# The mixer of a two-block network: its projection in three passes, weights streamed through four slots

## The reference

```python
proj = rms_norm(x) @ w_in                  # 1024 -> 2560: q, k, v, g, u
ret  = silu(g) * retention(rope(q), rope(k), v)   # chunks of 128 tokens, 8 heads
pool = (window_mean(u) - u) @ pool_w[g] * pool_scale   # 4 groups of 128 channels
h    = x + concat(ret, pool) @ w_out
# then h + moe(rms_norm(h)): logits, top 4 of 32 experts
```

## Time and profile before

| | us |
|---|---|
| median of 3 runs (lowest, highest) | 5710.15 (5708.48, 5718.44) |
| profiled execution | 5713.9 |
| its span, first to last instruction | 5712.2 |

### The profile page before, as it was taken

How to read it: one execution, slowest core, us unless ns; L and a number is a source line. 1 busy time by engine, 2 the same in 40 slices (tenths; PEclk the granted TensorE clock), 3 DMA queues, 4 the chain that set the end, 5 groups by cost and what they waited for, 6 DMA issues and landing times. The chain is left out here.

```text
span 5712.2 us, 77504 instructions
## 1 busy us (share of the span) xinstructions
PE 5329.2 (93%) x24921; PEld 3492.1 (61%) x24922; DVE 3181.3 (56%) x5954; ACT 2149.6 (38%) x3222; POOL 633.2 (11%) x865
## 2 busy tenths in 40 slices
PE   8999999499999999999999999789996599999788
PEld 4555555366666666666666666455654477777455
DVE  4434333567676767777777777443434544434176
ACT  3111111144444445555555555232222533333154
POOL 0000000100000000000000000100000199200000
PEclk9999999699999999999999999899998799999899
DMA  4112111356564647677777777333232300000433
GB/s 145 52 55 73 51 51 51 131 166 196 162 199 159 201 157 234 228 235 236 236 237 236 235 238 237 139 121 116 91 116 74 116 5 6 7 8 7 157 122 108
DMA packets 424923, 770.33 MB, mean 135 GB/s; under 512 B 57361, under 2 KB 142801, under 8 KB 423121
## 3 DMA queue, kind: packets, MB, share of 16 engines
q1 hardware_dynamic: 364304, 607.65, 31.8%
q10 hardware_dynamic: 33216, 87.05, 5.0%
q0 software_dynamic: 27280, 74.02, 3.9%
HBM read 630.45 MB, written 140.25 MB: 135 GB/s over the span
## 5 line engine op out<-in xcount | busy, mean ns | idle before, releaser
L1078 DVE TENSOR_TENSOR w_lo<-stage,w_hi 128x1024 bf16<-128x1024 f32 (+1 forms) x800 | 929.6, 1178 | 198.0 <-ACT w_hi L947 142.1
L947 ACT ACTIVATE w_hi<-stage 128x1024 fp32r<-128x1024 f32 (+1 forms) x800 | 791.8, 1017 | 582.9 <-PE GU L781 299.8
L778 PE MATMUL GU<-w_hi,x_hl 128*128 128x512 f32 x2048 | 859.9, 420 | 18.4 <-DVE x_hl L1083 7.6
L779 PE MATMUL GU<-w_hi,x_hl 128*128 128x512 f32 x2048 | 811.2, 396 | 0.0
L637 PE MATMUL PJ<-w_in_sb,xT 128*128 128x512 f32 x1200 | 544.3, 607 | 10.4 <-ACT xT L315 10.4
L781 PE MATMUL GU<-w_lo,x_bf 128*128 128x512 bf16 x2048 | 498.4, 381 | 0.0
L778 PEld LDWEIGHTS GU<-w_hi,x_hl 128*128 128x128 f32 x2048 | 386.6, 189 | 134.5 <-issue 28.2
L778 PE MATMUL Y<-w_hi,a_hl 128*128 128x512 f32 x1024 | 456.8, 446 | 0.0
L779 PEld LDWEIGHTS GU<-w_hi,x_hl 128*128 128x128 f32 x2048 | 387.4, 189 | 82.8
L779 PE MATMUL Y<-w_hi,a_hl 128*128 128x512 f32 x1024 | 404.4, 395 | 0.0
L637 PEld LDWEIGHTS PJ<-w_in_sb,xT 128*128 128x128 f32 x1200 | 228.7, 195 | 281.3 <-issue 267.2
(11 more groups left out here) (538 smaller groups left out, 8698.6 us busy)
## 6 DMA issues: line engine op xcount, KB each, us to landing
stage<-in_expert_w_gate_up_dram SPq DMA_DIRECT2D x512, 512.0 KB, 5.0
stage<-in_expert_w_down_dram SPq DMA_DIRECT2D x224, 512.0 KB, 5.7
expert_rows<-zero_y SPq DMA_DIRECT2D x16, 2048.0 KB, 9.9
b_gu<-in_expert_b_gate_up_dram ACTq DMA_DIRECT2D x128, 256.0 KB, 4.8
expert_rows<-acted ACTq DMA_DIRECT2D x64, 512.0 KB, 3.0
b_d<-in_expert_b_down_dram ACTq DMA_DIRECT2D x32, 512.0 KB, 8.0
stage<-in_expert_w_down_dram SPq DMA_DIRECT2D x64, 256.0 KB, 4.6
z<-z_sb SPq DMA_DIRECT2D x16, 992.0 KB, 5.6
```

The costliest lines, as they stand in the source:

```text
L778: pe.matmul(out, high(k), w_high(k), start=(k == first), stop=False)
L779: pe.matmul(out, low(k), w_high(k), start=False, stop=False)
L947: act.activation(w_hi[:, c, ks, :], staged, ACT.Copy).then_inc(s["hi_done"], 1)
L1078: dve.tensor_tensor(w_lo[:, c, ks, :], staged, w_hi[:, c, ks, :], ALU.subtract).then_inc(s["lo_done"], 1)
```

## The change

`w_in` is split once: its high part (float32r) stays in SBUF, its low part (bf16) is written to DRAM, and so is the scaled `w_out`, into whose lower rows the pooled map and its scale are multiplied once (four folds). Per tile 18 pieces of 512 KB are read back through four slots: 10 of the low part, 8 of the output map. x is split into high, low and bf16. The choice of experts moves behind rope on DVE, the state update behind ret, the bands into the first `body`; h gets a tile of its own. The diff, its core; `mixer_pieces` lists the pieces (t, j) in order, of which the last tile has only j 8 to 15:

```diff
+SLOTS_IN, PIECES = 4, 18
+OUT_FIRST, OUT_LAST = 8, 16
...
-w_in = sb("w_in_sb", [P, KD, PROJ])
-w_out = sb("w_out_sb", [P, KD, D])
-w_pool = sb("w_pool_sb", [P, GROUPS, P])
+w_hi = sb("w_in_hi", [P, KD, PROJ], F32R)
+stage = sb("mixer_stage", [P, 5 * 1024])
+slots = [stage[:, n * 1024:(n + 1) * 1024] for n in range(SLOTS_IN)]
+raw_in = [stage[:, n * PROJ:(n + 1) * PROJ] for n in range(2)]
+hnT = stage[:, 4096:5120].rearrange("p (k c) -> p k c", k=KD)
+late = sb("late", [P, 2 * D])
+h_sb, hn_sb = late[:, 0:D], late[:, D:]
+c_all = sb("c_all", [P, PROJ // 2])
+catT = c_all[:, 0:KD * P].rearrange("p (k c) -> p k c", k=KD)
+lo_in = [t[:, 0:PROJ // 2].bitcast(BF16) for t in (late, c_all)]
+out_rows = [stage[:, 4096:5120], h_sb]
...
-band0 = sb("band0", [P, GROUPS, P])
+band0 = late[:, 3 * BANK:].rearrange("p (g c) -> p g c", g=GROUPS)
...
-xT = sb("xT", [P, KD, P])
+x_hi, x_lo, x_bf = (sb(n, [P, KD, P], dt) for n, dt in (("mx_hi", F32R), ("mx_lo", F32R), ("mx_bf", BF16)))
...
-pooledT = sb("pooledT", [P, GROUPS, P])
-catT = sb("catT", [P, KD, P])
+w_pool, w_poolT = (vgu[:, 1, n * BANK:(n + 1) * BANK].rearrange("p (g c) -> p g c", g=GROUPS) for n in range(2))
...
+    def load_raw_in(k):
+        if k > 1:
+            sp.wait_ge(s["lo_made"], k - 1)
+        sp.dma_start(raw_in[k % 2], I["w_in"][0, k * P:(k + 1) * P, :]).then_inc(s[f"w_in_rows{k}"], 16)
+    def store_low_in(k):
+        sp.wait_ge(s["lo_made"], k + 1)
+        dst = S["w_in_lo"].rearrange("(n j) p (q c) -> j q p n c", j=2, q=4)[k // 4, k % 4]
+        sp.dma_start(dst, lo_in[k % 2].rearrange("p (n c) -> p n c", n=5)).then_inc(s[f"lo_stored{k % 2}"], 16)
+    def load_raw_out(k):
+        if k > 3:
+            sp.wait_ge(s["wo_made"], k - 3)
+        sp.dma_start(slots[k % 4], I["w_out"][0, k * P:(k + 1) * P, :]).then_inc(s[f"ring_in{k % 4}"], 16)
+    def store_out(k):
+        sp.wait_ge(s["wo_made"], k + 1)
+        dst = S["w_out_rows"].rearrange("(n j) p (q c) -> j q p n c", j=4, q=2)[k // 2, k % 2]
+        sp.dma_start(dst, out_rows[k % 2].rearrange("p (n c) -> p n c", n=2)).then_inc(s[f"wo_stored{k % 2}"], 16)
...
-    for k in range(KD):
-        sp.dma_start(w_in[:, k, :], I["w_in"][0, k * P:(k + 1) * P, :]).then_inc(s[f"w_in_rows{k}"], 16)
+    load_raw_in(0)
+    load_raw_in(1)
...
+    sp.dma_start(w_pool, I["pool_w"][0].rearrange("g c d -> c g d")).then_inc(s["pool_in"], 16)
     sp.wait_ge(s["x_loaded"], 16)
     load_x(1, 1)
+    for k in range(KD):
+        store_low_in(k)
+        if k + 2 < KD:
+            load_raw_in(k + 2)
+        elif k == KD - 2:
+            load_raw_out(0)
+            load_raw_out(1)
+    load_raw_out(2)
+    load_raw_out(3)
+    sp.dma_start(gain_moe[:, :], row(I["norm_moe_w"][0])).then_inc(s["router_in"], 16)
+    sp.dma_start(bias_rt[:, :], row(I["router_b"][0])).then_inc(s["router_in"], 16)
+    sp.dma_start(w_rt[:, :, :], I["router_w"][0].rearrange("(k p) e -> p k e", p=P)).then_inc(s["router_in"], 16)
+    for k in range(KD):
+        store_out(k)
+        if k < 4:
+            load_raw_out(k + 4)
...
+    def wait_used(t, j):
+        if j in (OUT_LAST - 3, OUT_LAST - 1):
+            sp.wait_ge(s["o_ps"], 2 * t + (1 if j == OUT_LAST - 3 else 2))
+        else:
+            ahead_of_it = j - (OUT_FIRST if t == TILES - 1 else 0) - (j > OUT_LAST - 3) - (j > OUT_LAST - 1)
+            sp.wait_ge(s["ring_free"], t * (PIECES - 2) + ahead_of_it + 1)
+    def load_piece(t, j):
+        n = piece_number(t, j)
+        if n >= SLOTS_IN:
+            wait_used(*pieces[n - SLOTS_IN])
+        else:
+            sp.wait_ge(s["wo_made"], n + 5)
+            if n == 0:
+                for b in range(2):
+                    sp.wait_ge(s[f"lo_stored{b}"], 16 * 4)
+                    sp.wait_ge(s[f"wo_stored{b}"], 16 * 4)
+        slot = n % SLOTS_IN
+        arrived = s[f"ring_in{slot}"]
+        if j < OUT_FIRST or j >= OUT_LAST:
+            m = j if j < OUT_FIRST else j - OUT_LAST + OUT_FIRST
+            sp.dma_start(slots[slot].bitcast(BF16), S["w_in_lo"][m]).then_inc(arrived, 16)
+        else:
+            m = j - OUT_FIRST
+            part, half, pair = m // 4, m % 4 // 2, m % 2
+            sp.dma_start(slots[slot], S["w_out_rows"][4 * half + 2 * (1 - part) + pair]).then_inc(arrived, 16)
+    def zero_rows(t, q):
+        sp.dma_start(unused[t][:, 8 * q:8 * q + 8, :],
+                     zero_y[:, :].unsqueeze(1).to_broadcast([P, 8, P])).then_inc(s["y_zeroed"], 16)
+    def next_x_and_store(t):
         sp.wait_ge(s["h_done"], t + 1)
-        sp.dma_start(h_t[bass.ds(t, 1)].squeeze(0), x_sb[:, par, :]).then_inc(s["h_stored"], 16)
+        if t + 2 < TILES:
+            load_x(t + 2, t % 2)
+        sp.dma_start(h_t[t], h_sb).then_inc(s["h_stored"], 16)
...
+    for t, j in pieces:
+        load_piece(t, j)
+        if t > 0 and j == 1:
+            next_x_and_store(t - 1)
+        if t > 0 and j == 3:
+            store_hn(t - 1)
+        if 4 <= j < 8:
+            zero_rows(t, j - 4)
+        if t == TILES - 1 and j == 8 + 1:
+            next_x_and_store(t - 1)
+            store_hn(t - 1)
+    for q in range(4):
+        zero_rows(TILES - 1, q)
+    next_x_and_store(TILES - 1)
+    store_hn(TILES - 1)
...
+    def copy_x(t):
         act.wait_ge(s["xT_ps"], t + 1)
-        act.activation(xT[:, 0:4, :], TR[:, 0:BANK], ACT.Copy).then_inc(s["xT_sb"], 1)
-        act.activation(xT[:, 4:8, :], TR[:, BANK:], ACT.Copy).then_inc(s["xT_sb"], 1)
+        for n in range(2):
+            act.activation(x_hi[:, 4 * n:4 * n + 4, :], TR[:, n * BANK:(n + 1) * BANK], ACT.Copy).then_inc(s["xT_sb"], 1)
+        act.wait_ge(s["xT_sb"], t * 2 + 2)
+        act.activation(x_bf[:, :, :], x_hi[:, :, :], ACT.Copy).then_inc(s["x_bf_ready"], 1)
+    def copy_c(t, part):
+        ks = slice(4, 8) if part == 0 else slice(0, 4)
+        act.wait_ge(s["pl_ps" if part == 0 else "ret_ps"], t + 1)
+        act.activation(catT[:, ks, :], SC[:, part * BANK:(part + 1) * BANK], ACT.Copy).then_inc(s["cat_ready"], 1)
...
+    def high_in(k):
         act.wait_ge(s[f"w_in_rows{k}"], 16)
-        act.activation(w_in[:, k, :], w_in[:, k, :], ACT.Copy, scale=gain_mix[:, k:k + 1]).then_inc(s["w_in_scaled"], 1)
+        act.activation(w_hi[:, k, :], raw_in[k % 2], ACT.Copy, scale=gain_mix[:, k:k + 1]).then_inc(s["w_hi_ready"], 1)
+    def scale_out(k):
+        if k > 1:
+            act.wait_ge(s[f"wo_stored{k % 2}"], k // 2 * 16)
+        if k < 4:
+            act.wait_ge(s[f"ring_in{k}"], 16)
+            act.activation(out_rows[k % 2], slots[k], ACT.Copy, scale=gain_out[:, k:k + 1]).then_inc(s["wo_made"], 1)
+        else:
+            act.wait_ge(s["fold_ps"], (k - 3) * 2)
+            for n in range(2):
+                last = act.activation(out_rows[k % 2][:, n * BANK:(n + 1) * BANK], fold_banks[k % 2][n], ACT.Copy)
+            last.then_inc(s["wo_made"], 1)
...
+    act.wait_ge(s["loads"], 32)
+    act.wait_ge(s["lo_made"], KD)
+    scale_out(0)
+    act.wait_ge(s["lo_stored0"], 16 * 4)
+    act.wait_ge(s["row_done"], 7)
+    scale_out(1)
     for n in range(5):
         evacuate(0, 0, n, False, first_banks[n])
+    for k in range(2, KD):
+        scale_out(k)
...
+    def low_x(t):
+        for n in range(2):
+            dve.wait_ge(s["xT_sb"], t * 2 + (n + 1))
+            dve.tensor_tensor(x_lo[:, 4 * n:4 * n + 4, :], TR[:, n * BANK:(n + 1) * BANK].rearrange("p (k c) -> p k c", k=4),
+                              x_hi[:, 4 * n:4 * n + 4, :], ALU.subtract).then_inc(s["x_lo_ready"], 1)
+    def low_in(k):
+        dve.wait_ge(s["w_hi_ready"], k + 1)
+        if k > 1:
+            dve.wait_ge(s[f"lo_stored{k % 2}"], k // 2 * 16)
+            dve.wait_ge(s["row_done"], k - 1)
+        dve.scalar_tensor_tensor(lo_in[k % 2], raw_in[k % 2], gain_mix[:, k:k + 1], w_hi[:, k, :],
+                                 ALU.mult, ALU.subtract).then_inc(s["lo_made"], 1)
...
+        if has_next:
+            low_x(t + 1)
...
+        if has_prev:
+            choose(t - 1)
...
         if not has_prev:
-            scale_w_out()
+            windows()
...
-        if has_prev:
-            place(t - 1, not isinstance(t, int) or t > 1)
...
+        if has_prev:
+            place(t - 1, not isinstance(t, int) or t > 1)
...
+    def arrived(half, c, j, skipped=0):
+        n = c * PIECES + j - skipped
+        pe.wait_ge(s[f"ring_in{n % SLOTS_IN}"], half * (16 * 2 * PIECES // SLOTS_IN) + 16 * (n // SLOTS_IN + 3))
+        return n % SLOTS_IN
+    def project(t, n, half, c):
+        if n == 0:
+            pe.wait_ge(s["xT_sb"], t * 2 + 1)
+            pe.wait_ge(s["x_lo_ready"], t * 2 + 1)
+        pe.wait_ge(s["proj_sb"], t * 5 + max(n - 1, 0))
+        out, cols = PJ[n % 2][:, :], slice(n * BANK, (n + 1) * BANK)
+        for k in range(4):
+            pe.matmul(out, x_hi[:, k, :], w_hi[:, k, cols], start=(k == 0), stop=False)
+            pe.matmul(out, x_lo[:, k, :], w_hi[:, k, cols], start=False, stop=False)
+        if n == 0:
```

(109 more changed lines are left out.)

220 lines of the change are left out of this document (106 added, 114 removed).

## The result

The changed kernel takes 5657.56 us (median of 4 runs, 5657.08 to 5659.24) where the kernel before takes 5713.96 beside it: ratio 0.9902 with a 95% interval of 0.9885 to 0.9919. It is 56 us faster. The prediction said 121 us, which is 5589, with 5560 to 5645 as its range.

What follows compares the result with a forecast made beforehand. The mixer was taken as bound by TensorE. Against 5713.9 us: tiles -135, body 0 -8, last tile -8, clock -8, head +38, together -121, giving 5593, or 5589 on the median's scale; range 5560 to 5645.

Steps and rivals of the forecast that it cites:

- Three passes, pooled map, end of the tile: Mixer tile: three-pass projections save 7.0 us, dropped pooled-map matmuls 0.94, filled waits 1.7; 62.8 becomes 53.2 us.
- The ring: Weight pieces streamed through four slots: a freed slot refills in about 4 us, needed after 5.15, so no wait.
- rival 1: Output projection: pieces land late by 2 to 4 us a tile, +32 to +64 us, 5621 to 5653; chance 0.17.
- 4.4 fits: Load of x in each tile: it must land 5.3 us after issue and takes 4.4, one piece ahead.
- DVE at the subtraction: End of a tile: DVE, queued behind three rope operations, reaches the subtraction for x's low part 0.7 us early.
- Rival 2: End of a tile: the wait for hn or x's low part ends last, 1 to 2 us a tile, 5605 to 5620; chance 0.08.
- The clock: TensorE in the tiles: with two waits gone, half of 17 us of excess comes back, 8 us.
- hn: End of a tile: hn is ready after 5.45 us, covered by a projection of 5.47; level, 0.04 us taken.
- Body 0: First tile body: gets the savings of projections and pooled map only, 8 us.
- The last tile: No projection as cover: earlier rope, state update and pooled map off the path save 8 us, between 3 and 10.
- The head: Weight preparation before the tiles: splitting and storing weights delays the second projection, +38 us, ends +25 and +55.

Runs made afterwards that it cites:

- four edits: Changed kernel with x loaded ahead of piece 1, low parts first, DVE's loop written out, first pieces between the head's last stores: 5601.65 us, 0.9798 of the kernel before.
- the tiles with and without: Changed kernel with x loaded first, low parts first and DVE's loop written out, POOL's scatter left out in even tiles: 768.4 us for the 14 tiles.
- shifted by 80: Changed kernel with 80 one-column copies on DVE in the head, so its unchanged loop begins 80 instructions later: 0.9847 of the kernel before.
- the small, unrolled kernel: Changed kernel with a quarter of the low-part bytes and half of the output map's, and DVE's loop written out: 5621.68 us, tiles 748.0 us.

## Why the prediction was wrong

**Three passes, pooled map, end of the tile: right.** These terms gave 53.2 us a tile. With late transfers and DVE's returns taken away a tile is 53.4 (748.0 / 14, with part of the weights left out), with four edits and all weights 54.0 (756.3 / 14), and 54.04 is in the changed kernel itself. A projection is 5.56 us against the 5.47 of the forecast.

**The ring: wrong, rival 1 in a smaller size.** The step took a latency of about 4 us for a slot that is needed again after 5.15, and so no wait. Its tight place was the turn inside the output projection, and the waits are not there. They stand at pieces 10 and 11, whose slots come free in projection 3 with 6.7 us in hand, and in the tile shown above piece 10 took 7.7 us. The forecast's rival had the ring late by 2 to 4 us a tile; it was late by 19.1 us in all, 1.4 a tile, and more by the clock. Two things made it late, and they are not parted in size. One is what rival 1 named, the bytes: with a quarter and half of them the waits are 2.4 us, the scatter in place, and x, h and hn landed in 6.3, 7.2 and 7.2 us instead of 4.4, 2.6 and 3.1. The other is POOL's queue. The scatter is in the kernel before, and the prediction did not price it, since nothing read DRAM behind it there; now pieces 10 and 11 are read behind it and crawl. That the scatter makes them crawl is shown by the tiles with and without; what inside the engines or the memory makes it so is not. Nor does the crawl always cost time: with four edits it is in every tile, and TensorE waits 0.3 us.

The Trainium skill (DMA: Bandwidth & Descriptors, Specifications) says that transfers under 512 bytes make the DMA engine read, modify and write. The scatter's words are of that kind; that reads behind them crawl the page does not say, and here they do.

**x: wrong.** "4.4 fits" in 5.3; it landed in 6.3 and TensorE waited 10.1 us for it, in all 14 tiles. Issued ahead of piece 1 it is waited for 2.0 us. The row had been taken from a queue that carried 3.7 MB a tile, not 13.

**DVE at the subtraction: wrong in 4 tiles of 14.** "0.7 us in hand" was worked out for a tile in which DVE's instructions are there. At every return of the loop its body was fetched again, and DVE stood for 5.1 us on average before the first instruction, which is rope with the subtraction behind it. Rival 2 named the subtraction, not this cause. No step of the prediction looked at where a loop lies: the change's new code in front moved DVE's from instruction 218 to 379, and that, not what the change computes, costs about 24 us (807.4 to 782.8 unrolled, to 784.0 shifted by 80).

**The clock: wrong.** Forecast was half of 17 us back, and in the changed kernel none is: 0.98 before and after, with 30.6 and 34.0 us at 0.50. The term had no place for new waits. Where the waits are gone all of it is back (1.00 over 14 tiles with four edits and with the small, unrolled kernel, with the transposes and 32-column matmuls still there). The prediction gave a rule of the Trainium skill (TensorE: Matmul & The Clock Gate, Part 4: PE-mode transpose) by which the drops would stay. They did not stay where the waits were gone.

**hn** was level as forecast: no wait on it in the loop. **Body 0** gave 7.9 us (57.0 to 49.1) for 8. **The last tile** gave 4.9 for 8. The wait for rope fell as forecast, from 6.80 to 2.00 us; but the wait for ret, ahead of its transposes, grew from 2.32 to 4.28, so TensorE came sooner and waited there. The 5.25 us on DVE before the transposes of hn are in both kernels.

**The head: +44 for +38**, inside its ends. The first projection ended at 68.5 for 66; the rest is in the chain of the output map, where TensorE waited 7.34 us on a raw row of w_out and the first fold took 3.54 us instead of 1.7, at the half clock.

The head with body 0 and the last tile missed 9 us, the tiles 54. The changed kernel's S0 and its part behind S14 with the tiles of the small, unrolled kernel between them would be 147.5 + 748.0 + 4700.3 = 5596 us, and the forecast for the span was 5591: it was the forecast of a kernel whose transfers are in time and whose loop stays. The four edits come near it with all the work done: their span is 5598.9 us.

## What to carry to other kernels

When a change makes an engine wait for DMAs that it did not use before, list every DMA of the other queues around the tightest one, however few bytes it has: behind a scatter of 512 words reads ran at a quarter of their speed or less. Take the landing time from a row whose queue carries as much as yours will. When code is added ahead of a hardware loop, look after the change for stops called "issue" at its returns and for instruction packets; moving the loop or writing it out took 24 us off the 14 tiles here, where the change as it stood gained 89. And ask of a resource that is delayed who may not overwrite its inputs.

## What the runs showed of the hardware that was not expected

- Behind four indirect DMAs of 128 words, the reads of 4 KB rows on the other queue ran at 25 to 150 GB/s for 3 to 9 us with the engines marked busy, though the scatter's own packets had ended some 5 us before: in all tiles with a scatter, and in none of the seven without. Issued among other reads, the scatter itself took 17.6 us from its last issue to its landing.
- Whether DVE's loop of some 300 instructions was fetched anew at each return hung on the place at which it began: 2 to 7 packets on the instruction queue or 26 to 27, and no stop over 0.4 us or one of up to 5.4 us (4.4 with the DMA engines at 0.45). 80 idle copies ahead of it took 25 us off the span (5655.2 to 5630.6).
- TensorE's longest waits, 3.3 to 3.7 us, were each followed by a stretch at 0.50 of the clock, as were three shorter ones down to 2.0 us; three of 2.0 to 2.7 us were not. Short waits do not rule it out: in the kernel before the stretches stand behind two waits of 0.69 us with transposes and 32-column matmuls between them, and with DVE unrolled two stretches follow a wait of 1.0 and 1.2 us for x at that place.
